# Which item of an expert is the full one, and the mask over its rows: a fused encoder layer with a mixture of experts

## Chip, cores and metric

One NeuronCore of a Trainium2 chip runs the whole layer in one launch. The metric is the device time in microseconds (us); lower is better. No other core takes part.

## The reference, cut to what matters

One layer: attention and a pooling mixer on 1024 tokens of width 1024, then a router that gives each token 4 of 32 experts, and a clamped SwiGLU expert on the rows it was given. Only the last part is touched:

```
logits = hf @ w_router + b_router;  topv, topi = top_k(logits, 4);  gates = softmax(topv)
for each expert e, for the rows of the tokens that chose e:
    g = min(xb @ w_gate[e] + b_gate[e], 7);  u = clip(xb @ w_up[e] + b_up[e], -7, 7)
    y = ((u + 1) * (g * sigmoid(1.702 * g))) @ w_down[e] + b_down[e]
    out[token] += y * gate
```

The three matrices of an expert are 1024x1024 in float32, so 12.6 MB per expert. The router's choice for these inputs, counted by evaluating the reference, gives the experts 0 to 31 this many rows: 135, 167, 108, 69, 133, 141, 71, 217, 126, 117, 91, 185, 46, 158, 74, 161, 157, 75, 210, 102, 117, 94, 60, 103, 182, 109, 128, 190, 148, 157, 111, 154. The order in which an expert's rows are computed does not change the result beyond rounding.

## The kernel before, in words

The kernel first does attention, output projection, router and the tables of the expert part (the first 620 us). Then all five engines run one hardware loop each over **items**. An item is up to 128 rows (CHUNK) of one expert; an expert with n rows has ceil(n / 128) items, 47 in all here. 15 experts have two items, 17 have one. The items stand in order of the expert, and the table of items gives for each the expert, the rank of its first row (`first`) and a number from which its **kind** follows. Before, the expression `shift = cnt - 128 * endi` makes this number the rank of the item's last row: the first item of an expert holds the remainder (1 to 128 rows), every later item is full.

TensorE (`item`, L1369 on) has four bodies of code, for items of at most 32, 64, 96 and 128 rows; it reads the number from the table and branches. The smaller kinds use column tiles of the array, so they need fewer cycles. I write "a 32", "a 64", "a 96" and "a 128" for items of these kinds. The kinds in the order before, one expert between bars (from the counts above, the remainder standing first):

32 128 | 64 128 | 128 | 96 | 32 128 | 32 128 | 96 | 96 128 | 128 | 128 | 96 | 64 128 | 64 | 32 128 | 96 | 64 128 | 32 128 | 96 | 96 128 | 128 | 128 | 96 | 64 | 128 | 64 128 | 128 | 128 | 64 128 | 32 128 | 32 128 | 128 | 32 128

An item on TensorE: bias (L1396, its first matmul), gate and up projections over the input rows k 0 to 3, then 4 to 7 (L1402), transposes of the hidden rows (L1412), down projection (L1427 for a 128, L1444 for a 64, L1465 for a 32, both of the last for a 96), among them the transposes of the next item's gathered rows (L1338, two halves) and the matmuls that find the rows of the item after it (L1330).

The weights have a single buffer, and SyncE reloads it in four parts as the **last item of an expert** lets go of them: both upper halves of gate and up (4 MB) after that item's k 0 to 3 (L439), both lower halves after its gate and up, half of w_down after half of its down projection, the rest after its end (L446):

```
done = sp.value_load(ends[0:1, bass.ds(e - 1, 1)], ...)
sp.wait_ge(s_k03, done)
```

VectorE (`with dve.Fori(0, MAX_ITEMS)`) at the start of item j makes the pick matrix for item j + 2: `item_slots` (L989 to L992) masks the ranks that lie beyond that item's last row and subtracts `first`, then `compare` (L996) compares with 0 to 127. After this `places` (L1012 on) waits for TensorE. Behind the SwiGLU work it waits until the rows of item j - 1 have been added in memory (`dve.wait_ge(s_added, j + 1)`), and then copies the places and gates of item j (L1121, L1122, L1065), which release ScalarE's scaling of the output rows (L765), moves the next item's rows (L1061), turns the found rows into numbers (L1006 to L1003) and chooses the next expert's bias row (L1023). The next item's first matmul waits for that last step. VectorE and ScalarE do four SwiGLU units for every kind, the unused ones too.

GpSimd gathers the rows of item j + 2 (L600) and adds the output rows of item j to memory with four indirect DMAs (L632), waits for all four and signals `s_added`.

Of the kernel before, what the change touches and what calls it, by code (L numbers as in the profile page):

```python
# [27 lines left out]
ALU = mybir.AluOpType  # L28
# [4 lines left out]
SEQ = 1024  # L33
# [13 lines left out]
CHUNK = 128  # L47
# [4 lines left out]
TABLE = MAX_ITEMS + 2  # L52
# [10 lines left out]
def encoder_kernel(nc, t, out):  # L63

    with ExitStack() as ctx:
# [3 lines left out]
        def sem(name):  # L69
            return ctx.enter_context(nc.semaphore(name))  # L70
# [107 lines left out]
        slot = Z[:, 18432:18688].rearrange("p (i e) -> p i e", i=TT)  # L178
# [7 lines left out]
        def small(cols):  # L186
            taken[0] += cols
            assert taken[0] <= 12288
            return Z[:, taken[0] - cols:taken[0]]
# [8 lines left out]
        b_r, cnt, nit, endi, shift, onese, is_exp, ejunk, iota_e = (small(EXPERTS) for _ in range(9))  # L198
        gsum, ginv, iota_p, iota_t, missing, limits = (small(c) for c in (8, 8, 1, 1, 1, 7))
        of_p, ofc, less = (small(c) for c in (4, 1, 1))  # L200
# [6 lines left out]
        col = small(8)  # L207
# [10 lines left out]
        items = small(3 * TABLE)[0:1, :].bitcast(I32)  # L218
        ends = small(EXPERTS)[0:1, :].bitcast(I32)
        bounds = Z[:, 17536:17536 + 3 * TABLE]  # L220
        last_of, first = bounds[:, 0:TABLE], bounds[:, 2 * TABLE:]
        total = small(1)[0:1, :].bitcast(I32)


# [93 lines left out]
        s_c2 = sem("router_constants_ready")  # L318
# [173 lines left out]
        def _(pl):  # L492
# [53 lines left out]
            for step_no in range(UNITS + 2):  # L546
                u = step_no - 2

                h, i = divmod(step_no, TT)
# [28 lines left out]
            exact = dict(allow_small_or_imprecise_dtypes=True)  # L578
            pl.iota(iota_e, [[1, EXPERTS]], base=0, channel_multiplier=0, **exact).then_inc(s_c2, 1)
            pl.iota(iota_p, [[1, 1]], base=0, channel_multiplier=1, **exact).then_inc(s_c2, 1)  # L580
            pl.iota(iota_t, [[1, 1]], base=CHUNK, channel_multiplier=CHUNK, **exact).then_inc(s_c2, 1)
            pl.iota(iota_c, [[1, CHUNK]], base=0, channel_multiplier=0, **exact).then_inc(s_c2, 1)
            pl.iota(limits, [[CHUNK, 7]], base=CHUNK, channel_multiplier=0, **exact).then_inc(s_c2, 1)
            pl.iota(missing, [[1, 1]], base=SEQ + 1, channel_multiplier=1, **exact).then_inc(s_c2, 1)
# [195 lines left out]
        def _(dve):  # L780
            step = [0]

            def link(ins):
                step[0] += 1
                ins.then_inc(s_dve, 1)
                dve.wait_ge(s_dve, step[0])
# [200 lines left out]


            def item_slots(chain, e, n):  # L989
                own = slot[:, :, e].rearrange("p i e -> p (i e)")  # L990
                chain(dve.scalar_tensor_tensor(col, own, last_of[:, n], own, ALU.is_le, ALU.mult))
                chain(dve.tensor_scalar(col, col, first[:, n], None, ALU.subtract))  # L992

            def compare(dst=pickT):
                for i in range(TT):
# [26 lines left out]
            def choose(e):  # L1022
                dve.tensor_scalar(chosen[0:3 * EXPERTS, :], onesb[0:3 * EXPERTS, :],  # L1023
                                  of_row[0:3 * EXPERTS, e], None, ALU.mult).then_inc(s_chosen, 1)
# [15 lines left out]
            dve.tensor_copy(ends, endi[0:1, :]).then_inc(s_tab, 1)  # L1040
            link(dve.tensor_copy(total, endi[0:1, EXPERTS - 1:EXPERTS]))

            link(dve.scalar_tensor_tensor(shift, endi, -float(CHUNK), cnt, ALU.mult, ALU.add))
            link(dve.tensor_scalar(is_exp, endi, iota_p, None, ALU.is_le))
            link(dve.tensor_reduce(of_p[:, 0:1], is_exp, AX_X, ALU.add))
            link(dve.tensor_scalar(of_p[:, 0:1], of_p[:, 0:1], float(EXPERTS - 1), None, ALU.min))
            link(dve.tensor_scalar(is_exp, iota_e, of_p[:, 0:1], None, ALU.is_equal))
            link(dve.tensor_tensor_reduce(out=ejunk, in0=is_exp, in1=shift, scale=1.0, scalar=0.0, op0=ALU.mult,
                                          op1=ALU.add, accum_out=ofc))
            link(dve.tensor_tensor(of_p[:, 1:2], ofc, iota_t, ALU.add))  # L1050
            link(dve.tensor_scalar(less, of_p[:, 1:2], 33.0, None, ALU.is_lt))
            link(dve.scalar_tensor_tensor(of_p[:, 2:3], of_p[:, 1:2], 97.0, less, ALU.is_lt, ALU.add))
            link(dve.tensor_scalar(of_p[:, 3:4], of_p[:, 1:2], 1.0 - CHUNK, 1.0, ALU.add, ALU.max))
            for n in range(4):
                dve.tensor_scalar(diag[:, n * TABLE:(n + 1) * TABLE], ident[:, 0:TABLE], of_p[:, n:n + 1], None,
                                  ALU.mult).then_inc(s_diag, 1)
# [15 lines left out]
            e1 = dve.value_load(items[0:1, 1:2], min_val=0, max_val=EXPERTS - 1)  # L1072
            kind0 = dve.value_load(items[0:1, 2 * TABLE:2 * TABLE + 1], min_val=0, max_val=KINDS - 1)
            item_slots(link, slice(0, 1), slice(0, 1))
            compare(pick0)
            dve.wait_ge(s_pick, 2)
            item_slots(link, bass.ds(e1, 1), slice(1, 2))
            compare()
            choose(slice(0, 1))
# [8 lines left out]
            dve.sem_inc(s_ucl, UNIT)  # L1088

            LOOP0 = step[0]  # L1090
            PER = 11
            n_items = dve.value_load(total, min_val=EXPERTS, max_val=MAX_ITEMS)
            with dve.Fori(0, MAX_ITEMS) as j:
                with dve.If(j < n_items):
                    local = [0]

                    def chain(ins):
                        local[0] += 1
                        ins.then_inc(s_dve, 1)
                        dve.wait_ge(s_dve, j * PER + (LOOP0 + local[0]))  # L1100

                    e1 = dve.value_load(items[0:1, bass.ds(j + 1, 1)], min_val=0, max_val=EXPERTS - 1)
                    e2 = dve.value_load(items[0:1, bass.ds(j + 2, 1)], min_val=0, max_val=EXPERTS - 1)
                    kind = dve.value_load(items[0:1, bass.ds(j + (2 * TABLE + 1), 1)], min_val=0, max_val=KINDS - 1)
                    item_slots(chain, bass.ds(e2, 1), bass.ds(j + 2, 1))
                    compare()
                    places(chain, j + 1, kind)
# [21 lines left out]
                    choose(bass.ds(e1, 1))  # L1129
                    assert local[0] == PER  # L1130

# [469 lines left out]
```

## Time and profile before

| what | us |
|---|---|
| median of 3 runs | 2505.13 (2503.92 to 2511.53) |
| the profiled execution, its own time | 2503.77 |
| its span | 2502.0 |
| loop over the items, first matmul of the first item to ScalarE's first output scaling of the last | 1845.15 (619.90 to 2465.05) |

The profile tells when each engine was busy with what and what released it after a wait. A row of the order of time reads: start, duration, engine, line, operation, and in brackets how long the engine had been idle and what ended it; "issue" means that nothing the profile shows was waited for.

### The profile page before, as it was taken

The numbers are of one execution on the slowest core, as the hardware profiler recorded it, in microseconds if no ns is written. First come the engines' busy times: TensorE is split into PE (matmuls) and PEld (weight loads), VectorE is DVE, ScalarE is ACT, GpSimd is POOL, SyncE is SP. The second block draws the span as 40 slices with busy tenths as digits, with TensorE's granted clock in tenths as the row PEclk, the third lists the DMA queues.
The fourth block names the chain that finished last, engine by engine and source line by source line (L and its number), as shares of the span: only waits on it lengthen the run. The fifth ranks groups of instructions, "written<-read, shape, count | busy, mean of one in ns | idle before, by whom it ended". The sixth has DMA issues, their size and how long they took to land.

```text
span 2502.0 us, 30088 instructions
## 1 busy us (share of the span) xinstructions
PE 2254.2 (90%) x9757; PEld 1054.0 (42%) x9758; DVE 859.1 (34%) x2563; ACT 475.5 (19%) x1006; POOL 508.0 (20%) x442
## 2 busy tenths in 40 slices
PE   8999899995789889999989899899998999989984
PEld 4444677553334344334433334334443344334431
DVE  2012888345323233232233323323222323233233
ACT  1000787210111111111111111111111101111112
POOL 1031463102121112211121221221112111222121
PEclk9999999996889999999989999999998999999997
DMA  7000011414347856938859694593889668567754
GB/s 267 9 1 29 39 68 51 158 65 188 113 141 288 329 184 198 344 98 330 310 167 342 205 342 155 194 339 104 332 305 366 223 230 302 163 222 235 270 182 151
DMA packets 149247, 502.78 MB, mean 201 GB/s; under 512 B 10170, under 2 KB 34767, under 8 KB 147631
## 3 DMA queue, kind: packets, MB, share of 16 engines
q1 hardware_dynamic: 113200, 446.79, 46.8%
q0 software_dynamic: 34128, 50.35, 10.2%
q10 hardware_dynamic: 1874, 5.02, 0.5%
q8 instruction: 31, 0.51, 0.1%
q14 instruction: 14, 0.11, 0.0%
HBM read 463.82 MB, written 42.50 MB: 202 GB/s over the span
## 4 chain that ended last, share of the span: by engine, by line
PE 82%; DVE 7%; issue 6%; DMA 2%; POOL 2%; ACT 2%; DVEq 0%; ACTq 0%; POOLq 0%
PE psum L1402 40%; PE psum L1427 13%; PE psum L1179 9%; PE psum L1237 4%; PE psum L1444 3%; PE psum L1465 2%; PE psum L1338 2%; PE psum L1396 2%; PE psum L1412 2%; DMA weights<-in_w_down 1%; DVE work L880 1%; POOL osq L563 1%; PE psum L1330 1%; PE psum L1226 1%; PE psum L1295 1%
## 5 line engine op out<-in xcount | busy, mean ns | idle before, releaser
L1402 PE MATMUL psum<-weights,work 128*128 128x512 f32 (+2 forms) x3520 | 1065.2, 617 | 0.0
L1402 PEld LDWEIGHTS psum<-weights,work 128*128 128x128 f32 (+2 forms) x3520 | 399.1, 158 | 530.3 <-issue 523.3
L1427 PE MATMUL psum<-weights,work 128*128 128x512 f32 x768 | 347.4, 595 | 0.0
L600 POOL DMA_INDIRECT work<-normed_rows,work x49 | 49.6, 1011 | 1408.8 <-DVE work L1003 1097.7
L632 POOL DMA_INDIRECT residual_rows<-work x188 | 294.8, 1568 | 123.2 <-ACT work L765 72.6
L758 ACT ACTIVATE work<-work 128x256 f32<-128x256 f32 x188 | 77.3, 411 | 809.2 <-DVE work L1111 809.2
L1179 PE MATMUL psum<-weights 128*128 128x512 f32 x512 | 220.5, 593 | 2.6 <-DVE weights L823 2.6
L1427 PEld LDWEIGHTS psum<-weights,work 128*128 128x128 f32 x768 | 140.0, 190 | 141.4 <-issue 137.9
L1012 DVE TENSOR_REDUCE work<-psum 128x8 f32 x48 | 8.8, 184 | 485.9 <-PE psum L1352 485.9
L1111 DVE TENSOR_SCALAR work<-psum 128x256 f32<-128x256 f32 x188 | 79.5, 423 | 272.0 <-PE psum L1402 272.0
L760 ACT ACTIVATE work<-psum 128x256 f32<-128x256 f32 x188 | 71.6, 381 | 443.3 <-PE psum L1412 443.3
L1396 PE MATMUL psum<-work 96*128 96x512 bf16 (+2 forms) x220 | 58.6, 414 | 104.0 <-issue 104.0
L1179 PEld LDWEIGHTS psum<-weights 128*128 128x128 f32 x512 | 97.0, 190 | 125.0 <-issue 121.9
L765 ACT ACTIVATE work<-psum,work 128x256 f32<-128x256 f32 x188 | 73.8, 475 | 342.6 <-PE psum L1427 255.5
L1061 DVE TENSOR_TENSOR work<-psum,gains 128x512 f32<-128x512 f32 x96 | 66.4, 691 | 168.0 <-PE psum L1338 161.5
L1444 PE MATMUL psum<-weights,work 128*64 128x512 f32 x480 | 109.0, 595 | 3.3 <-ACT work L760 3.3
L1237 PE MATMUL psum<-weights 128*128 128x512 f32 x256 | 111.8, 594 | 0.0
L1115 DVE TENSOR_TENSOR work<-work 128x256 f32<-128x256 f32 x188 | 80.0, 426 | 83.8 <-ACT work L758 81.4
L996 DVE TENSOR_SCALAR work<-work 128x128 bf16<-128x128 f32 x400 | 86.4, 299 | 1.8
L1117 DVE SCALAR_TENSOR_TENSOR work<-work 128x256 f32<-128x256 f32 x188 | 79.9, 425 | 6.5
L880 DVE CUSTOM_DVE_ANT_0 work<-psum,weights 128x1024 f32<-128x1024 f32 x64 | 78.1, 1221 | 6.0 <-PE psum L1226 5.4
L833 DVE TENSOR_SCALAR work<-psum 128x512 f32<-128x512 f32 x16 | 11.1, 691 | 199.3 <-PE psum L1179 199.3
(199 smaller groups left out, 1795.8 us busy)
## 6 DMA issues: line engine op xcount, KB each, us to landing
weights<-in_w_gate SPq DMA_DIRECT2D x64, 2048.0 KB, 7.8
weights<-in_w_up SPq DMA_DIRECT2D x64, 2048.0 KB, 12.4
weights<-in_w_down SPq DMA_DIRECT2D x64, 2048.0 KB
x<-in_x SPq DMA_DIRECT2D x16, 512.0 KB, 6.6
weights<-in_w_in SPq DMA_DIRECT2D x8, 1024.0 KB, 15.6
residual_rows<-x SPq DMA_DIRECT2D x9, 512.0 KB, 2.6
normed_rows<-work ACTq DMA_DIRECT2D x9, 512.0 KB, 2.7
bias_rows_repeated<-bias_rows SPq DMA_DIRECT2D x4, 1024.0 KB, 9.7
```

Source lines behind the costliest of these rows:

```text
L632: pl.indirect_dma_start(acc_d[:, :], bass.IndirectOffsetOnAxis(dest[:, b:b + 1], 0), yrow[:, b * BLK:(b + 1) * BLK], None, compute_op=ALU. ...
L880: dve.tensor_tensor_reduce(out=prob[:, u % SETS, m, :], in0=PS[:, 2 * m * HALF:(2 * m + 2) * HALF], in1=bias[:, h, at:at + SEQ], scale=1.0 ...
L996: last = dve.tensor_scalar(dst[:, i, :], iota_c, col[:, i:i + 1], None, ALU.is_equal)
L1111: dve.tensor_scalar(gmin[:, b, :], bank(b, BLK), LIMIT, None, ALU.min).then_inc(s_gm, 1)
L1115: dve.tensor_tensor(sig[:, b, :], gmin[:, b, :], sig[:, b, :], ALU.mult).then_inc(s_sg, 1)
L1117: dve.scalar_tensor_tensor(hid[:, b, :], ucl[:, b, :], 1.0, sig[:, b, :], ALU.add, ALU.mult).then_inc(s_hid, 1)
L1179: return pe.matmul(bank(4 + n % 4), lhs, rhs, start=(k == 0), stop=(k == DT - 1))
L1237: mm = pe.matmul(bank(n % 4), mixT[:, c, i * P:(i + 1) * P], w_out[:, c, q * HALF:(q + 1) * HALF], start=(c == 0), stop=(c == DT - 1))
L1396: pe.matmul(out, chosen[0:3 * EXPERTS, 0:cols], bgu[:, :, blk * BLK:(blk + 1) * BLK], start=True, stop=False)
L1402: mm = pe.matmul(out.rearrange("p (m n) -> p m n", m=2), xT[:, k, lo:lo + cols], wgu[:, :, k, blk * BLK:(blk + 1) * BLK], start=False, sto ...
L1427: mm = pe.matmul(bank(4 + h), actT[:, k, :], wdn[:, k, h * HALF:(h + 1) * HALF], start=False, stop=(k == DT - 1))
L1444: mm = pe.matmul(PS[64 * h:64 * h + 64, 4 * HALF:5 * HALF], actT[:, 2 * b + s, 64 * c:64 * c + 64], wdn[:, k, h * HALF:(h + 1) * HALF], st ...
```

## The change

The table of items now starts from the first row of the expert's first item: `shift` is 128 times the number of items before the expert, `first` is 1 + 128 * (p - items before), and the number from which the kind follows is the count of the expert's rows that are left when item p begins, clamped to 0..1024. So an expert's first item is full when it has more than one, and its last holds the remainder. Ranks beyond an item's 128 rows now give a column of 128 or more, which no comparison meets, so the masking instruction of `item_slots` goes. The order of kinds is now:

128 32 | 128 64 | 128 | 96 | 128 32 | 128 32 | 96 | 128 96 | 128 | 128 | 96 | 128 64 | 64 | 128 32 | 96 | 128 64 | 128 32 | 96 | 128 96 | 128 | 128 | 96 | 64 | 128 | 128 64 | 128 | 128 | 128 64 | 128 32 | 128 32 | 128 | 128 32

```diff
-        last_of, first = bounds[:, 0:TABLE], bounds[:, 2 * TABLE:]
+        first = bounds[:, 2 * TABLE:]
...
-            pl.iota(iota_t, [[1, 1]], base=CHUNK, channel_multiplier=CHUNK, **exact).then_inc(s_c2, 1)
+            pl.iota(iota_t, [[1, 1]], base=0, channel_multiplier=CHUNK, **exact).then_inc(s_c2, 1)
...
             def item_slots(chain, e, n):
-                own = slot[:, :, e].rearrange("p i e -> p (i e)")
-                chain(dve.scalar_tensor_tensor(col, own, last_of[:, n], own, ALU.is_le, ALU.mult))
-                chain(dve.tensor_scalar(col, col, first[:, n], None, ALU.subtract))
+                chain(dve.tensor_scalar(col, slot[:, :, e].rearrange("p i e -> p (i e)"), first[:, n], None,
+                                        ALU.subtract))
...
-            link(dve.scalar_tensor_tensor(shift, endi, -float(CHUNK), cnt, ALU.mult, ALU.add))
+            link(dve.tensor_tensor(shift, endi, nit, ALU.subtract))
+            link(dve.tensor_scalar(shift, shift, float(CHUNK), None, ALU.mult))
+            link(dve.tensor_tensor(cnt, cnt, shift, ALU.add))
...
-            link(dve.tensor_tensor(of_p[:, 1:2], ofc, iota_t, ALU.add))
+            link(dve.tensor_tensor_reduce(out=ejunk, in0=is_exp, in1=cnt, scale=1.0, scalar=0.0, op0=ALU.mult,
+                                          op1=ALU.add, accum_out=of_p[:, 1:2]))
+            link(dve.tensor_tensor(of_p[:, 1:2], of_p[:, 1:2], iota_t, ALU.subtract))
+            link(dve.tensor_scalar(of_p[:, 1:2], of_p[:, 1:2], 0.0, float(SEQ), ALU.max, ALU.min))
...
-            link(dve.tensor_scalar(of_p[:, 3:4], of_p[:, 1:2], 1.0 - CHUNK, 1.0, ALU.add, ALU.max))
+            link(dve.tensor_scalar(ofc, ofc, -1.0, 1.0, ALU.mult, ALU.add))
+            link(dve.tensor_tensor(of_p[:, 3:4], ofc, iota_t, ALU.add))
...
-            PER = 11
+            PER = 10
```

On VectorE, the start of the item loop before: the loads of the table, the mask (L991), the subtraction (L992), the eight comparisons and the wait for TensorE's matmuls.

```order
507 L1104 TENSOR_LOAD work
508 L1104 ISA x2
509 L991 ISA
510 L991 SCALAR_TENSOR_TENSOR work<-work 128x8
511 L1100 ISA
512 L992 ISA
513 L992 TENSOR_SCALAR work<-work 128x8
514 L1100 REGISTER_ALU
515 L996 TENSOR_SCALAR work<-work 128x128 x8
```

The same place in the changed kernel, whose lines are numbered one less here.

```order
510 L1109 TENSOR_LOAD work
511 L1109 ISA x2
513 L990 ISA
514 L990 TENSOR_SCALAR work<-work 128x8
515 L1105 ISA
516 L995 TENSOR_SCALAR work<-work 128x128 x8
```

One instruction of 128x8 is gone from each item; nothing else on VectorE has moved in the loop. On VectorE, the making of the item table ahead of the loop, before:

```order
453 L1041 CAST work<-work 1x1
454 L1043 SCALAR_TENSOR_TENSOR work<-work 128x32
455 L1044 TENSOR_SCALAR work<-work 128x32
459 L1048 ISA work<-work 128x32
460 L1048 ISA work 128x1
461 L1050 TENSOR_TENSOR work<-work 128x1
462 L1051 TENSOR_SCALAR work<-work 128x1
463 L1052 SCALAR_TENSOR_TENSOR work<-work 128x1
464 L1053 TENSOR_SCALAR work<-work 128x1
465 L1055 TENSOR_SCALAR work<-ident,work 128x66 x4
```

The same place in the changed kernel:

```order
454 L1042 TENSOR_TENSOR work<-work 128x32
455 L1043 TENSOR_SCALAR work<-work 128x32
456 L1044 TENSOR_TENSOR work<-work 128x32
463 L1051 ISA work<-work 128x32
464 L1051 ISA work 128x1
465 L1053 TENSOR_TENSOR work<-work 128x1
466 L1054 TENSOR_SCALAR work<-work 128x1
469 L1057 TENSOR_SCALAR work<-work 128x1
470 L1058 TENSOR_TENSOR work<-work 128x1
471 L1060 TENSOR_SCALAR work<-ident,work 128x66 x4
```

The first expression has become three instructions, a second masked sum (L1051, an instruction and the reading of its accumulator) and a clamp (L1054) have come in, and one instruction has become two (L1057, L1058). The other engines have the same instructions; which of TensorE's bodies of code an item takes is decided by the table at run time.

## Rows read from the trace of the kernel before

**Rows 1.** The page: shares of the chain of work that ended last, by engine.

```profile
PE 82%; DVE 7%; issue 6%; DMA 2%; POOL 2%; ACT 2%; DVEq 0%; ACTq 0%; POOLq 0%
```

**Rows 2.** Item starts on TensorE in order of time: 96, 96, 128, 128.

```profile
1635.43 0.41 PE L1396 MATMUL psum<-work 96*64 96x512 bf16 x2
1674.75 0.61 PE L1396 MATMUL psum<-work 96*64 96x512 bf16 x2 [3.73 <-issue]
1715.36 0.39 PE L1396 MATMUL psum<-work 96*128 96x512 bf16 x1 [3.33 <-issue]
1761.91 0.38 PE L1396 MATMUL psum<-work 96*128 96x512 bf16 x1
```

**Rows 3.** Item starts on TensorE in order of time: 128, 64, 128, 32, 128, 32.

```profile
2092.76 0.38 PE L1396 MATMUL psum<-work 96*128 96x512 bf16 x1
2137.70 0.41 PE L1396 MATMUL psum<-work 96*64 96x512 bf16 x2
2167.60 0.61 PE L1396 MATMUL psum<-work 96*128 96x512 bf16 x1 [3.65 <-issue]
2215.29 0.40 PE L1396 MATMUL psum<-work 96*32 96x512 bf16 x4
2236.82 0.61 PE L1396 MATMUL psum<-work 96*128 96x512 bf16 x1 [3.68 <-issue]
2284.04 0.40 PE L1396 MATMUL psum<-work 96*32 96x512 bf16 x4
```

**Rows 4.** Item starts on TensorE: a 64 behind a 96, then a 128.

```profile
1266.07 0.64 PE L1396 MATMUL psum<-work 96*64 96x512 bf16 x2 [3.56 <-issue]
1298.91 0.60 PE L1396 MATMUL psum<-work 96*128 96x512 bf16 x1 [3.64 <-issue]
```

**Rows 5.** Down projection's first matmul in small items: all grouped (count, busy, mean ns, idle before), and one.

```profile
L1459 PE MATMUL psum<-work 96*32 96x256 bf16 x64 | 4.9, 295 | 13.5 <-DMA weights<-in_w_down 8.4 <-ACT work L760 5.1
...
1393.60 0.41 PE L1459 MATMUL psum<-work 96*32 96x256 bf16 x4 [5.15 <-DMA weights<-in_w_down]
```

**Rows 6.** Item starts on TensorE: the 128 behind that waiting 32, and the next item.

```profile
1403.33 0.39 PE L1396 MATMUL psum<-work 96*128 96x512 bf16 x1 [2.90 <-issue]
1448.28 0.41 PE L1396 MATMUL psum<-work 96*64 96x512 bf16 x2
```

**Rows 7.** VectorE in the loop: mask, and the wait behind it; count, busy, mean ns, idle before.

```profile
L991 DVE SCALAR_TENSOR_TENSOR work<-work 128x8 f32 x47 | 10.9, 232 | 125.2 <-issue 125.2
L1012 DVE TENSOR_REDUCE work<-psum 128x8 f32 x47 | 8.7, 184 | 485.2 <-PE psum L1352 485.2
```

**Rows 8.** ScalarE in order of time: output scaling of the 32 that starts at 2215.29.

```profile
2230.99 1.20 ACT L765 ACTIVATE work<-psum,work 128x256 f32<-128x256 f32 x3 [1.25 <-DVE work L1065]
```

**Rows 9.** Last adding DMA in that 32, no weights in flight: issue, and time to landing.

```profile
2223.39 1.56 POOL L632 DMA_INDIRECT residual_rows<-work  x1 [0.30 <-issue]
residual_rows<-work POOLq DMA_INDIRECT x1, 4.0
```

**Rows 10.** SyncE's issue at 1353; adding DMA's landing at 1353.8 and 1381; page's weight landing.

```profile
1353.55 0.38 SPq L439 DMA_DIRECT2D weights<-in_w_gate  x1
residual_rows<-work POOLq DMA_INDIRECT x1, 7.8
residual_rows<-work POOLq DMA_INDIRECT x1, 8.9
weights<-in_w_up SPq DMA_DIRECT2D x64, 2048.0 KB, 12.4
```

**Rows 11.** Starts of the second, fourth, sixth item; the page's queue of TensorE's instruction loads.

```profile
650.64 0.60 PE L1396 MATMUL psum<-work 96*128 96x512 bf16 x1 [11.04 <-issue]
734.11 0.61 PE L1396 MATMUL psum<-work 96*128 96x512 bf16 x1 [10.53 <-issue]
831.28 0.41 PE L1396 MATMUL psum<-work 96*64 96x512 bf16 x2 [4.62 <-issue]
q8 instruction: 31, 0.51, 0.1%
```

## The prediction

> **What bounds the kernel now.** I read the page first: TensorE has 82% of the chain that ended last [rows 1], and VectorE, ScalarE, GpSimd and the DMA queue each have slack on average. So the question is how long TensorE takes from the first matmul of one item to that of the next, and how this interval depends on what stands before it. The second view is therefore the order of time on TensorE at the starts of items (L1396). I write a|b for the interval of an a that stands behind a b. A 128|128 takes 2137.70 - 2092.76 = 44.9 us, a 64|128 29.9, a 128|64 47.7, a 32|128 21.5 (2236.82 - 2215.29), a 128|32 47.2 [rows 3]. A 96|96 takes 40.6 and a 96|128 39.3, a 128|96 46.5 [rows 2], a 64|96 32.8 [rows 4]. The reader is to see two things. Each kind has its own length, so moving an item inside its expert changes nothing at first. But an item behind a smaller one starts after a pause of 3.3 to 3.7 us that nothing in the profile ended: it comes behind the choice of the next expert's bias, which a 128 prepares ahead of its last matmuls and the smaller kinds only after them. And it runs longer: a 128 by 1.6 us (behind a 96) or by 2.3 to 2.8 (behind a 32 or 64), a 96 by 1.3, a 64 by 2.9.
>
> The third view groups what ended the waits inside items. For weights, the first matmul of a small item's down projection waits 8.4 us in all, 5.15 of it in one 32; the usual releaser is ScalarE, 5.1 us over all others [rows 5].
>
> **The change part by part.** The sum is made against the profiled execution (2503.77 us; the median shown is 1.4 higher); minus is faster.
>
> *The mask.* One instruction of 232 ns per item, with its hand-over some 0.4 us; 47 of them are 18 us of VectorE's time. But behind the comparisons VectorE waits for TensorE's L1352, 485 us over 47 items, 10 each [rows 7]. That wait grows by 0.4 each: **0**. Without this cover it would be -18.
>
> *Weights that came late.* A remainder that stands first meets weights whose last part is still under way; standing last it uses what its expert has long had. Two 32s hold the 8.4 us, of which about 1.5 would be spent anyway, so -6.9. But the 128 behind the first of them took only 1448.28 - 1403.33 = 44.9 us after a pause of 2.9 [rows 6], without the 2.3 that a 128|32 pays; I take the same for the other, and give back 2.3 each and some tenths of pause. Net **-1.5** (ends -6.9 and 0).
>
> *Who stands behind whom.* From the two lists of kinds: before, 14 128s stand behind a 32 or 64 and 2 behind a 96; 3 64s, 2 96s and 2 32s stand behind a smaller item, the first item aside. After, it is 10 and 7 128s, 2 64s, 3 96s and no 32. With 2.3, 1.6, 2.9, 1.3 and for a 32 1.8 (about the mean of these, an estimate), the extras are 32.2 + 3.2 + 8.7 + 2.6 + 3.6 = 50.3 before and 23.0 + 11.2 + 5.8 + 3.9 = 43.9 after: **-6** (ends -8 and -4, as a 96 behind a 32 or a 64 behind a 64, which no row shows, may cost 1 more each, and the 128's extra is between 2.3 and 2.8).
>
> *The end of the loop.* The last item is now a 32, and the last needs no pause behind it. ScalarE's output scaling begins 2230.99 - 2215.29 = 15.7 us after the start of a 32 [rows 8], 5.8 before the next start would be; behind a last 128 there is no such rest. **-6**. What comes after the loop is the same.
>
> *The adding of the rows.* This is the price of the new order. While a 32 runs behind a 128, GpSimd adds the rows of that 128, and VectorE may pass its wait for this at L1121, the first of three copies of 0.2 us ahead of the scaling at +15.7: at +15.0. Before, the 32 is an expert's first, so the next weights aren't asked for: the last of the four DMAs is issued at +8.1 and lands 4.0 later, at +12.1, and VectorE isn't held up [rows 9]. After, the 32 is its expert's last, and SyncE asks for the next expert's gate and up, 8 MB, from about +4 on. In a 64 where this was so already (weights asked for at 1353.55) the last adding DMA took 7.8 us, in another stretch with weights 8.9 [rows 10]. That makes +15.9 to +17.0, and some tenths until VectorE knows of it: it is 1 to 2.5 late. Late next are the scaling, the move of the next rows and so the next item's start, one behind the other. Seven 32s have this (the eighth is the last item, with no weights behind it): 7 to 17. I take 1.6 each, near the 64's row, since that is the same place in the program: **+11**. A 64 or 96 reaches L1121 later and keeps its cover. The low end is 0, if the four DMAs get through as they did without weights.
>
> *Do the next weights come in time behind a remainder?* A 32 lets the first quarter go 4 us after its start and ends its interval at 21.5; the 4 MB land in 12.4 [rows 10], at +16.4: 5 us of cover. All 12.6 MB took 40 us from issue to use in the tightest stretch (1353.55 to 1393.60) [rows 5, 10], so they are there at +44. The down projection begins when about two thirds of a 128 are over and 0.6 of a smaller kind (gate and up against the whole of its matmuls): for a 128 at 21.5 + 31 = +52, for a 96 at +46. The tightest is expert 12's 64 behind expert 11's 64: asked for at +7.5, there at +47.5, wanted at 29.9 + 19 = +49. **0**; without the cover it is 2 us at that one place.
>
> *Loading TensorE's code.* The starts of the second, fourth and sixth item have idle times of 11.04, 10.53 and 4.62 us, where a 128 behind a 32 or 64 has 3.7 later on and one behind a 128 none; TensorE's code came in 31 loads, 0.51 MB together [rows 11]. Over those the three hold 7.3 + 6.8 + 4.6 = 19 us. Each was among the first entries into its body by a jump. They stay, in another order. New is that the first item of all is a 128, whose code lies behind all other bodies, while a 32's follows on the loop's head. The nearest row is the sixth item's: **+4** (ends -7, if one of the two dear entries into the 128 goes with this, and +11, if it costs what they did). The Trainium skill ("Runtime: NRT & Kernel Launch", Instruction fetch mechanics) says that a taken branch to a page outside a window of two pages waits for the page's load. By that rule every change of kind would stall all through the loop, which is rival 2's direction; the trace shows such stalls in the first six items and none in the later rows.
>
> *The table.* Six instructions more for it and two masks fewer, 0.23 us each as the mask: 1.4 - 0.5 = **+1**. TensorE waits for this chain ahead of the first item.
>
> Sum: 0 - 1.5 - 6 - 6 + 11 + 0 + 4 + 1 = **+2.5**. That is 2506.3 for the profiled execution and on the median 2508 us.
>
> **The rivals.**
> 1. *The adding of rows stays covered.* For it: without weights in flight it has 3 us to spare. Against: both stretches with weights. The sum is then 2.5 - 11 = -8.5, 2497 on the median; with no new stall for code -12.5, 2493. This is the other side of no change. It decides from where the last DMA takes under 6.5 us. 0.14.
> 2. *Code loads cost much more.* If the first 128 pays 11 and the first 32 and the first 96 behind it pay 4.6 each, it is 16 over my sum: 2524; with one of these alone 2513 to 2515. For it: no jump from a 128 back into a 32 comes among the first six items before. Against: the third item entered the 64 from a 128 without a stall among those rows. 0.15.
> 3. *The remainder is too short a cover for the weights.* A 32 gives 18 us to a load of 40, where the full item gave 42. If adding, gathering and weights slow each other so that the first 4 MB take more than 17.5 us, each us beyond it costs 7, once for each 32: at 20 us it is +17, 2525. Against: 12.4 is the median over loads with adding in flight too. 0.08.
> 4. *The mask was on the path:* -18, 2490. Only if VectorE's start of an item set TensorE's pace, which its 10 us of wait exclude. 0.02.
>
> The forecast has 0.61.
>
> **How the numbers follow.** 0.3%, 7.5 us, is about what a measurement of this kernel can tell from no change. The forecast's own range is 2500 to 2515. The whole range reaches to 2496 for rival 1 and to 2520 for rivals 2 and 3. Faster than 2497.6: most of rival 1 and rival 4, 0.15. Slower than 2512.6: rivals 2 and 3 and a little of the forecast (the adding at its high end), 0.25. Within: 0.60.
>
> **What would show it right or wrong.** In the changed kernel L1121 should stand behind a wait for the adding DMA in seven 32s, 1 to 2.5 us each, and their intervals be 22.5 to 24 instead of 21.5; no wait for w_down should be left; a 128|96 should be 46.5, seven times; the last scaling should come 15.7 us after its item's start. The first item's start shows the code's part. Wrong would be: waits for w_gate or w_up at L1402, pauses of "issue" above 4 us beyond the sixth item, or no wait at L1121.

## The result and the profile after

The changed kernel takes 2525.58 us (2524.68 to 2531.07, 4 runs) against 2504.97 before: ratio 1.0081, 95% interval 1.0059 to 1.0104. It is slower by 20.6 us, where I had forecast 2.5 to 3 more and a range up to 2520. The profiled execution took 2524.68, its span is 2522.9: 20.9 more than before. I explain these 20.9.

In all rows below lines of VectorE up to L1042 are one lower than before, from L1066 on five higher: L1121 is now L1126, L1396 is L1401, L1402 is L1407. The page of the changed kernel, with the rows that answer to [rows 1, 7, 11] and the landing of weights:

```profile
span 2522.9 us, 29951 instructions
PE 2253.9 (89%) x9757; PEld 1055.9 (42%) x9758; DVE 854.3 (34%) x2520; ACT 475.0 (19%) x1006; POOL 506.3 (20%) x442
q8 instruction: 32, 0.52, 0.1%
PE 79%; DVE 7%; issue 7%; DMA 3%; POOL 3%; ACT 2%; DVEq 0%; ACTq 0%; POOLq 0%
L1011 DVE TENSOR_REDUCE work<-psum 128x8 f32 x48 | 8.8, 184 | 509.5 <-PE psum L1357 509.5
weights<-in_w_up SPq DMA_DIRECT2D x64, 2048.0 KB, 14.3
```

TensorE does the same work (9757 matmuls) and has less of the chain, 79% instead of 82%; GpSimd and DMA each have one point more. The first place to look is the wait that the prediction named. The grouped view of VectorE's L1126 says how often the engine stood still ahead of it and for whom:

```profile
L1126 DVE CAST work<-work x47: 160/163/171, 659.3 to 2483.2; 128x4 uint32<-128x4 f32 x47
its engine sat idle before it (us, times) until:
  POOLq L637: 17.8, 7
```

Before, nobody held it up there:

```profile
L1121 DVE CAST work<-work x47: 161/161/165, 636.7 to 2451.0; 128x4 uint32<-128x4 f32 x47
its engine sat idle before it (us, times) until:
who waited for it (us, times):
```

L637 is GpSimd's signal that an item's rows are added. One of the seven items in the order of time: its start on TensorE, the last adding DMA's issue, its landing time, the late L1126, the next start.

```profile
2280.87 0.40 PE L1401 MATMUL psum<-work 96*32 96x512 bf16 x4
2288.92 1.55 POOL L632 DMA_INDIRECT residual_rows<-work  x1 [0.30 <-issue]
residual_rows<-work POOLq DMA_INDIRECT x1, 8.8
2297.91 0.17 DVE L1126 CAST work<-work 128x4 uint32<-128x4 f32 x1 [1.94 <-POOLq L637]
2304.40 0.61 PE L1401 MATMUL psum<-work 96*128 96x512 bf16 x1 [3.63 <-issue]
```

The DMA is issued at +8.1 as before [rows 9], but lands 8.8 later instead of 4.0 (in the seven it is 8.8 to 9.8); L1126 runs at +17.0 instead of +15.0, and the next item starts at +23.5 instead of +21.5. The six 32s with such a follower, the second item aside, took 24.6, 24.5, 24.7, 24.6, 23.5 and 23.5.

The other place is the first five items. TensorE's starts there, with the pause that nothing ended, as in [rows 11]:

```profile
626.27 0.61 PE L1401 MATMUL psum<-work 96*128 96x512 bf16 x1 [8.43 <-issue]
703.92 0.61 PE L1401 MATMUL psum<-work 96*128 96x512 bf16 x1 [9.56 <-issue]
792.88 0.61 PE L1401 MATMUL psum<-work 96*128 96x512 bf16 x1 [15.34 <-issue]
844.38 0.41 PE L1401 MATMUL psum<-work 96*64 96x512 bf16 x2 [4.16 <-issue]
```

These are the first, third, fifth and sixth item. Over what such starts cost otherwise (3.9 at the first, 3.7 behind a small item, 0 behind a 128) the pauses hold 4.5 + 5.9 + 11.6 + 4.2 = 26.2 us; before it was 18.7. The loads of code stop where these pauses stop. Of the 32 loads 17 come ahead of the loop; the window from 618 to 900 us has the other 15, the last at 885.0, and no later window has one (before, 14 in the loop, the last at 871.9):

```profile
q8 instruction: 15, 0.25, 0.3%
```

### The profile page after: what moved, and what is told of

It reads as the page before. It is cut to its first block, busy times and chain, and to the rows that moved or that the text cites. A ratio compares the mean times of both kernels' runs of the same rounds, so it can differ in the third digit from the quotient of the medians.

```text
span 2522.9 us, 29951 instructions
## 1 busy us (share of the span) xinstructions
PE 2253.9 (89%) x9757; PEld 1055.9 (42%) x9758; DVE 854.3 (34%) x2520; ACT 475.0 (19%) x1006; POOL 506.3 (20%) x442
## 4 chain that ended last, share of the span: by engine, by line
PE 79%; DVE 7%; issue 7%; DMA 3%; POOL 3%; ACT 2%; DVEq 0%; ACTq 0%; POOLq 0%
PE psum L1407 39%; PE psum L1432 13%; PE psum L1184 9%; PE psum L1242 4%; PE psum L1449 3%; DMA residual_rows<-work 3%; PE psum L1343 2%; PE psum L1401 2%; DVE work L880 1%; PE psum L1417 1%; POOL residual_rows L632 1%; PE psum L1470 1%; POOL osq L563 1%; PE psum L1231 1%; PE psum L1335 1%
## 5 line engine op out<-in xcount | busy, mean ns | idle before, releaser
L1407 PE MATMUL psum<-weights,work 128*128 128x512 f32 (+2 forms) x3520 | 1066.6, 612 | 0.0
L1407 PEld LDWEIGHTS psum<-weights,work 128*128 128x128 f32 (+2 forms) x3520 | 400.9, 158 | 529.1 <-issue 521.9
L1011 DVE TENSOR_REDUCE work<-psum 128x8 f32 x48 | 8.8, 184 | 509.5 <-PE psum L1357 509.5
L1401 PE MATMUL psum<-work 96*128 96x512 bf16 (+2 forms) x220 | 58.6, 408 | 109.8 <-issue 109.8
L1066 DVE TENSOR_TENSOR work<-psum,gains 128x512 f32<-128x512 f32 x96 | 66.4, 691 | 162.6 <-PE psum L1343 156.1
L1343 PE MATMUL psum<-ident,work 128*128 128x128 f32 x384 | 62.7, 288 | 39.2 <-DVE work L1066 39.2
## 6 DMA issues: line engine op xcount, KB each, us to landing
weights<-in_w_down SPq DMA_DIRECT2D x64, 2048.0 KB, 11.6
```

Of the source, the lines that this page charges most:

```text
L1343: mm = pe.transpose(bank(7, P, c * P), xg[:, k * P:(k + 1) * P], ident[:, :])
L1401: pe.matmul(out, chosen[0:3 * EXPERTS, 0:cols], bgu[:, :, blk * BLK:(blk + 1) * BLK], start=True, stop=False)
L1407: mm = pe.matmul(out.rearrange("p (m n) -> p m n", m=2), xT[:, k, lo:lo + cols], wgu[:, :, k, blk * BLK:(blk + 1) * BLK], start=False, sto ...
```

## The experiments

The theories: **A**, the adding DMAs are slowed by the next expert's weights, and the small item's follower waits for them; **code**, the loading of TensorE's code by far jumps; against them **B**, it is the place in the expert and not the weights, and the mask or weight waits.

**1. The mask put back.**

```diff
-                chain(dve.tensor_scalar(col, slot[:, :, e].rearrange("p i e -> p (i e)"), first[:, n], None,
-                                        ALU.subtract))
+                own = slot[:, :, e].rearrange("p i e -> p (i e)")
+                chain(dve.scalar_tensor_tensor(col, own, 0.0, own, ALU.is_ge, ALU.mult))
+                chain(dve.tensor_scalar(col, col, first[:, n], None, ALU.subtract))
...
-            PER = 10
+            PER = 11
```

> The changed kernel with one instruction of 128x8 put back where the mask stood (it multiplies the ranks by 'not negative', so it changes no value). If the mask's time is hidden behind VectorE's wait for TensorE (10 us per item), the time stays at 2525 (within 3). If VectorE's start of an item is on the path, it is 47 x 0.4 = 18 us more, 2543.

2528.23 us (2525.9 to 2529.95), ratio to before 1.0093, 1.0076 to 1.0110. Its interval overlaps that of the changed kernel (1.0059 to 1.0104): no 18 us. In the traces the loop is as long with the mask as without it, 1841.6 us from the first item's start to the last's against 1841.9; the 2.2 us between the profiled executions lie ahead of the first item. The grouped wait shows where the time went; it stands at 494.9 where the changed kernel has 509.5, over 48 instructions:

```profile
L1012 DVE TENSOR_REDUCE work<-psum 128x8 f32 x48 | 8.8, 184 | 494.9 <-PE psum L1358 494.9
```

That is 0.3 us per item: the mask takes its own time out of a wait, as said.

**2 and 3. Nearly no weights in flight, in both orders.**

```diff
-                    load_gu(m, 0, bass.ds(e, 1))
+                    tiny_gu(m, 0, bass.ds(e, 1))
...
+            def tiny_gu(m, half, e):
+                src = wgu_d[m][:, e, 4 * half, 0:8].rearrange("p e n -> p (e n)")
+                sp.dma_start(wgu[:, m, 4 * half, 0:8], src).then_inc(s_wk[half], 16)
```

(and the same for the other three loads). Both kernels leave out the weights of all experts but the first; they are there for their times alone.

> The changed kernel, but from the second expert on each weight load brings 8 columns of one row block only (left out: the weights of all experts but the first; the work on every engine stays). Theory A, the adding DMAs are late because the next expert's weights are in flight: the wait ahead of L1126 (17.8 us over 7 items) is gone and a 32 behind a 128 takes 21.5 us again instead of 23.5 to 24.8; about 19 us less than the changed kernel's 2525, so 2506. Rival B, it is the position in the expert or the order of GpSimd's work, not the weights: intervals of 24 us remain, 2524.

> The kernel before, with the same cut of the weight loads. Its late w_down (8.4 us of wait in two items) goes, but the items behind start colder: 2503 by both theories. Theory A then has the two orders 3 us apart once no weights are in flight (code loads +9, end of the loop and colder starts -8 to -10, table +1), rival B 20.

One execution each: 2500.06 (span 2498.2) and 2496.32 (span 2494.6). The orders are 3.6 us apart instead of 20.9. Without weights the new order gains 24.7 and the old one 7.4. In the new order the wait ahead of the three copies is gone, and a 32 behind a 128 takes 21.5 to 21.9 again. The same item as above, with L1409 as its first matmul and L1134 as VectorE's first copy:

```profile
2262.00 0.40 PE L1409 MATMUL psum<-work 96*32 96x512 bf16 x4
2277.01 0.16 DVE L1134 CAST work<-work 128x4 uint32<-128x4 f32 x1
2283.48 0.60 PE L1409 MATMUL psum<-work 96*128 96x512 bf16 x1 [3.62 <-issue]
```

Theory A holds and B falls. The new order came out 6 us below what I had expected of it, and the old one 7 us below its 2503, and in good part for the same reason. A second thing came out there, which I had not looked for: the pauses of the first items became shorter too. The third and fifth item:

```profile
701.91 0.61 PE L1409 MATMUL psum<-work 96*128 96x512 bf16 x1 [8.14 <-issue]
787.14 0.61 PE L1409 MATMUL psum<-work 96*128 96x512 bf16 x1 [11.09 <-issue]
```

With weights in flight it was 9.56 and 15.34, and the sixth item's pause fell from 4.16 to 2.53. The 15.34 is no accident of one execution: experiments 1, 4 and 8, which have weights and the same code, show 15.51, 15.36 and 15.38. In the old order the long pauses of the second and fourth item come when hardly any weights are asked for, and they barely changed (11.04 and 10.53 became 10.41 and 10.20); the sixth's, with weights under way, went from 4.62 to 2.08. In the fourth item three pages of code are loaded with weights and without; each is under way for about 1 us either way. But they start 29.6, 35.5 and 38.9 us after the item's start instead of 27.6, 31.9 and 34.6, which makes the 4.3 us. What holds up their start is not shown.

Ahead of the first item these executions are less alike: with the same code and nearly the same pause it starts at 629.1 here, at 626.3 in the changed kernel.

**4. VectorE's wait moved off TensorE's path, new order.**

```diff
-                    dve.wait_ge(s_added, j + 1)
-                    chain(dve.tensor_copy(dest, nextitem[:, 0:4]))
-                    chain(dve.tensor_copy(dgate, nextitem[:, 4:8]))
-                    shift_places(j + 1)
                     move_xT(j + 1)
...
                     choose(bass.ds(e1, 1))
+                    dve.wait_ge(s_added, j + 1)
+                    chain(dve.tensor_copy(dest, nextitem[:, 0:4]))
+                    chain(dve.tensor_copy(dgate, nextitem[:, 4:8]))
+                    shift_places(j + 1)
+                    dve.tensor_copy(less, new)
```

The last line is a copy of one column that nothing reads later; it takes 0.15 us.

> The changed kernel with VectorE's wait for the added rows and the three copies behind it moved behind the move of the next rows, the row numbers and the choice of the expert. TensorE's next item then no longer hangs on that wait. Theory A: the 17.8 us of wait leave the path, and each small item (22 that have a follower) is 0.6 us shorter as the three copies leave it too: 2525 - 19 - 13 = 2493. Rival C, the stall is only passed on (GpSimd adds the small item's rows later, and the next item hangs on its gather): little gain, 2515 or more.

2497.77 us (2494.27 to 2500.05), ratio 0.9967, 0.9953 to 0.9981: 28 less than the changed kernel, and faster than the kernel before. The gain is near what was worked out, 32, so the stall is not just passed on (rival C). A 32 behind a 128 takes 20.8 to 21.9. Where it fell short shows in the grouped waits, a row that the changed kernel does not have (L1403 is the first matmul here):

```profile
PE psum L1403 <- DMA weights<-in_w_up: 20.9, 5, 4.7
```

and in one of those starts:

```profile
2283.57 0.39 PE L1403 MATMUL psum<-work 96*128 96x512 bf16 x1 [3.71 <-DMA weights<-in_w_up]
```

The next expert's first weights now land last, after a pause of 3.7 that would be there anyway. So rival 3 (a remainder is too short a cover) is a real second limit that lay just behind the first; the five pauses are 3.7 to 4.7, so it costs up to 1 us per item here.

**5. The same move in the old order.** The diff is that of experiment 4.

> The kernel before (remainder first, mask in), with the same move of VectorE's wait and copies as in the changed kernel's version that reached 2498. In the old order that wait never held, so by theory A only the three copies leave the path: 23 x 0.6 = 13 us, 2492, and the old order stays 5 us ahead of the new one. Rival D, the move helps for another reason than the wait: then it gives the old order as much as the new one, 27 us, 2478.

2494.72 us (2492.17 to 2497.29), ratio 0.9954, 0.9937 to 0.9971: 10 to 11 less than before. The move gives the new order 28 and the old one 11. The part that both have I put down to the three copies (13 expected; most of the small items are 0.7 us shorter); the other 17 fit the wait that only the new order has, 17.8 us. Rival D, the same gain in both orders, falls.

**6 and 7. The full item's code first.**

```diff
-                    with pe.If(n_tok < 97):
-                        with pe.If(n_tok < 33):
...
+                    with pe.If(n_tok > 96):
+                        item(j, e, e2, 128)
+                    with pe.Else():
+                        with pe.If(n_tok < 33):
```

> The changed kernel with TensorE's body for full items placed first in the loop's code instead of last; no other edit. If the loading of code by a far jump is what the first items pay for (start of the first item 5 us late, 6, 12 and 5 us in the second, fourth and fifth), the first item starts at 621 instead of 626.3 and the loop loses 5 to 20 us: 2510 to 2520. If those delays have another cause, nothing moves: 2525.

> The kernel before with the same placing of the full items' body. Here the first item is a 32, whose code then lies behind the full body. By the code theory its start (619.9) gets 4 to 6 us later, and the dear entries into the full body (7 us each, two) go: 2495 to 2508. If the cause is another: 2505.

New order: 2506.50 us (2503.13 to 2507.7), ratio 1.0002, 0.9988 to 1.0015: 19 less than the changed kernel and below the 2510 to 2520 I had expected. Old order: 2491.80 (2489.78 to 2494.91), ratio 0.9943, 0.9925 to 0.9961: 13 to 14 less than before. It is the largest single gain in the old order, and lies below the 2495 to 2508 I had expected. The loads of code, new order first (32 before), then old order (31 before):

```profile
q8 instruction: 27, 0.44, 0.1%
```

```profile
q8 instruction: 25, 0.41, 0.1%
```

And the first start in the new order, where the full item's code now follows on the loop's head; the pause is 3.83 instead of 8.43:

```profile
622.32 0.61 PE L1401 MATMUL psum<-work 96*128 96x512 bf16 x1 [3.83 <-issue]
```

In the old order the first start moved the other way, from 619.91 with 3.93 to this, as the code theory has it for a 32 whose code has moved to the far side:

```profile
625.14 0.62 PE L1396 MATMUL psum<-work 96*32 96x512 bf16 x4 [8.18 <-issue]
```

The loop won it back at the second and fourth item (7.25 and 7.22 instead of 11.04 and 10.53), and the sixth item's 4.62 is gone. But the code of the first items is not the whole gain. At the start of the eighth item the old order is 9.2 us ahead, of 13.4 in the span, and the new one 16.6 of 20.6; in the new order the second item's wait for the adding, 3.1, is gone too. The rest comes later, where no code is loaded: in the new order the pause ahead of a 128 behind a 96 is 2.9 us instead of 3.3, and three of the seven then take 44.9 instead of 46.6. The first 5.4 us of one of them, in the changed kernel and here; behind the times of the five engines stand TensorE's granted clock, the share of the DMA engines and GB/s:

```profile
1155.20:1160.60 5.40, 5.40 (x10) 2.26 (x11) 2.19 (x9) 0.00 (x0) 4.49 (x4) 0.68 1.00 388
1137.40:1142.80 5.40, 5.40 (x14) 2.54 (x15) 2.20 (x9) 0.00 (x0) 4.66 (x3) 1.00 1.01 391
```

The clock stayed at 1.00 (2.4 GHz), and TensorE got through 14 matmuls instead of 10. So the place of the code also sets how long the pause in front of an item is, and a shorter pause can leave the clock up; behind the other four of the seven, with the same pause, it was 0.68 to 0.74.

**8. The next weights held back until the rows are added, new order.**

```diff
                 sp.wait_ge(s_k03, done)
+                sp.wait_ge(s_added, done)
```

> The changed kernel, but SyncE asks for the next expert's first weights only when the rows of the item before the expert's last are added (for a 32 some 8 us later than now; for larger last items hardly ever later). Theory A: no wait is left ahead of L1126, since the adding DMAs run alone; but the first 4 MB then land at +25 of a 32 behind a 128, later than the next start at +21.5, so 3 to 4 us move to a wait for weights at the next item: intervals of 25, time 2522 to 2530. Rival B (not the weights): the wait ahead of L1126 stays at 17 us in all and the weight waits come on top, 2545.

2534.18 us, one execution. The wait ahead of the copies is gone, as A says and against B; the same time and more stands at the next expert's start:

```profile
PE psum L1402 <- DMA weights<-in_w_up: 60.2, 7, 10.3
```

The upper end of what I expected was 2530. Six of the pauses are 8.0 to 8.7 us, 3.7 of which are there in any case (the 10.3 is the third item's, which loads code too), and the 32s take 25.8 to 26.6. So one after the other, the adding of 0.5 MB of rows and the first 4 MB of weights do not fit in a small item's 21 us; beside each other, as in experiment 4, they overrun it by 1 us at most.

**9 and 10. Both edits, in both orders.** The diffs are those of experiments 4 and 6.

> The old order with both edits, VectorE's wait and copies moved and the full items' body first. If wait and code loads are separate causes the gains add: 2505 - 11 - 14 = 2480.

> The new order with both edits. Separate causes: 2525.5 - 28 - 19 = 2479, level with the old order under the same edits or a few us ahead (no late w_down, the last item a 32). If code and wait were the whole of the change's price, the two orders differ by less than 5 us. If the new order has a further cost, such as waits for w_gate and w_up at the next expert's start, it stays 5 to 10 us behind.

Old order: 2473.32 us (2470.25 to 2477.35), ratio 0.9871, 0.9856 to 0.9886, 7 us better than the sum of the two gains; where these 7 come from is not shown. New order: 2479.26 (2477.69 to 2486.39), ratio 0.9907, 0.9893 to 0.9921, as the sum said. The two intervals stay just apart, and by medians the old order is 6 us faster, which was the case of a further cost. The two profiled executions cannot show it: they are the old order's slowest and the new one's fastest, with spans of 2475.6 and 2475.9. The new order is the one with waits for weights at L1403, 24.8 us in 6 items; 3.6 or so of each would be a pause anyway, so some 3 us of the 6 could be theirs, and the rest stays open:

```profile
PE psum L1403 <- DMA weights<-in_w_up: 24.8, 6, 4.6
```

The best kernel of the case is number 9, the old order with both edits, 32 us or 1.3% faster than before. It needs neither the new order nor the dropped mask.

## Why the prediction was wrong

Its terms again, with what the two traces give for each (us, plus is slower):

| term | forecast | measured |
|---|---|---|
| the mask | 0 | 0 |
| weights that came late | -1.5 | -1.5 |
| who stands behind whom | -6 | -2.5 |
| the end of the loop | -6 | -4 |
| the adding of the rows | +11 | +19.5 |
| cover for the next weights | 0 | 0 |
| code | +4 | +7.5 |
| the table | +1 | +1.8 |
| sum | +2.5 | +20.8 of 20.9 |

**The step that failed most is "I take 1.6 each, near the 64's row".** The mechanism, its place, the number of items and the later price were right: seven waits, L1121, one after the other to the next start. The size was not. The waits are 1.9 to 3.1, 2.5 each (17.8 in 7), and six intervals grew by 145.4 - 6 x 21.5 = 16.4, so 2.7 each; with the second item's 3.1 it is 19.5. That lies not only over my +11 but over the upper end of the term, 17. I had two rows for the landing, 7.8 and 8.9, and took the lower because it is "the same place in the program", a 64 whose weights are asked for 0.3 us ahead of the last adding DMA. The changed kernel has that place five times, and there the last DMA lands 8.9 to 9.9 after its issue. One of them, its start, the request for weights, the adding DMA and its landing:

```profile
2203.96 0.41 PE L1401 MATMUL psum<-work 96*64 96x512 bf16 x2
2211.75 0.38 SPq L439 DMA_DIRECT2D weights<-in_w_gate  x1
2212.01 1.55 POOL L632 DMA_INDIRECT residual_rows<-work  x1 [0.30 <-issue]
residual_rows<-work POOLq DMA_INDIRECT x1, 9.9
```

So the 7.8 was no price of the place but one low row, and in the 32s it is 8.8 to 9.8. The 7.8 came where the last part of the weights before had been asked for only 7.7 us ahead of the new ones; whether that made it lower, no run shows. Nor was the 4.0 of [rows 9] quite without weights: between 2223.3 and 2224 their queue still moved 0.07 MB. Experiment 2 has 3.7 to 3.9 with nearly none. Experiments 2, 4 and 8 each take away one side of the meeting, weights or wait, and the stall goes.

**Code: right in sign, half in size.** I added the cheapest row, 4.6 at one start. The first start paid just that (4.5), but the entries behind it paid too: 5.9, 11.6 and 4.2, where before it was 7.3, 6.8 and 4.6. The 15.34 at the fifth item is the surprise. Experiment 2 shows that 4.3 of it come from weights in flight, since 11.09 remain without. I had counted the code's loads as a price of the jump alone and not as transfers that cost more beside weights. Experiments 6 and 7 move nothing but the place of the code and gain 19 and 14, so the place of the code is a cause; the difference of these gains, 5 to 6, is near the +7.5, but 3.1 of the 19 are the second item's wait, and a part of both gains lies behind the first items. Which page is loaded when, and why a second entry into the full body pays again, stays open. The page of the Trainium skill that I cited ("Runtime: NRT & Kernel Launch", Instruction fetch mechanics) says that a taken branch out of a window of two pages waits for its page. By that every change of kind would stall; the trace does not agree: no page is loaded after 885.0, while the kinds change through 40 more items.

**Who stands behind whom.** My 1.3 for a 96 behind a small item came from behind a 96; behind a 32 it is 1.8 to 2.5 (41.2, 40.7 and 41.4 against 38.9), and the pause ahead of it is 4.0. A 128 behind a 32 takes 47.4 to 47.8, so 2.6 and not 2.3. The seven 128s behind a 96 took 46.5 to 46.7 as forecast. The starts of such a 96 and of the item behind it:

```profile
1028.41 0.64 PE L1401 MATMUL psum<-work 96*64 96x512 bf16 x2 [4.02 <-issue]
1069.63 0.39 PE L1401 MATMUL psum<-work 96*128 96x512 bf16 x1 [3.31 <-issue]
```

Before, the extras are 49.3 (forecast 50.3), after 46.8 (forecast 43.9). What an extra is, the windows show: the first 5.4 us of a 128 behind another 128, then of the 128 that starts at 2304.40 behind a pause of 3.63. The columns are those of the windows in experiments 6 and 7:

```profile
2159.00:2164.40 5.40, 5.40 (x15) 2.56 (x14) 1.89 (x9) 2.85 (x5) 2.53 (x2) 1.00 1.02 408
2304.40:2309.80 5.40, 5.40 (x7) 2.33 (x8) 2.21 (x9) 0.00 (x0) 4.49 (x4) 0.51 1.03 409
```

Behind the pause TensorE has a granted clock of 0.51, near its lower level (1.2 GHz), and gets through 7 matmuls, where it does 15 at 1.00 (2.4 GHz). That costs about half of these 5.4 us.

**The end of the loop.** The last scaling does start 15.7 after the item's start, at 2483.89. But what follows is not the same, as I had said. In order of time on GpSimd:

```profile
2487.87 1.01 POOL L600 DMA_INDIRECT work<-normed_rows,work  x1 [10.07 <-DVE work L1002]
2489.18 1.58 POOL L632 DMA_INDIRECT residual_rows<-work  x1 [0.30 <-issue]
```

GpSimd's loop gathers for item j + 2 before it adds the rows of item j, and in a 32 the row numbers for that gather come after the scaling. So the adding starts 5.3 us behind the scaling, where behind a last 128 it was 2.4. Until the end of the span it is 39.0 instead of 36.9.

**The table.** The +1.8 is 626.27 - 619.91 less the 4.5 of code. It is read from one execution each, and the start of the first item moves by up to 3 us between executions of the same code up to there (625.7 to 629.1), so one execution hardly measures a term of this size.

**Right:** the mask (experiment 1); no wait for weights in any item of the changed kernel; no late w_down. But the cover was nearly gone: the first 4 MB landed 20.0 to 21.0 us after such a 32's start and not at +16.4, because the load took 15.4 to 16.3 from the issue of its second half and not 12.4. Against the +21.5 at which the next start used to come that is 0.5 to 1.5 us of cover instead of 5. Rival 3 was wrong for this kernel by that little: with the adding and the copies off the path it shows (experiments 4 and 10). Rival 1 is dead, and rival 2 is right in part. Rivals 2 and 3 had 2524 and 2525, which is what was measured, but not what happened: the time came from the adding and, less, from code and from who stands behind whom. The chances had 0.25 for slower, and the reasons for it stood in the text; the low choice within the bounds of the largest term, and bounds from two rows, kept the range too short.

## What to carry to other kernels

A transfer that a wait hangs on has two prices, alone and beside the traffic that the change moves next to it. Where only two rows show the second, they are no bounds: here both the lower and the higher lay below most of what came. Let the sum be tried with more than the higher one. A pause of a few us on TensorE has a second price too, the lower clock behind it. Where a small piece of work must cover loads, a scatter and bookkeeping, ask for each in which order they land; taking the latest away shows the next. And first ask whether the wait has to be on the path at all: moving it behind the work that the other engine needs gave 28 us in the new order and 11 in the old.

## What the hardware showed that I had not expected

The last of an item's adding DMAs (four of 128 rows of 1 KB) landed 3.7 to 4.0 us after its issue with few or no weights in flight (experiment 2, [rows 9]), and 7.8 to 9.9 when the next 8 MB of weights were asked for ahead of it (the kernel before and the changed one). Pauses in which TensorE's code is loaded were longer beside weights (15.34 us with, 11.09 without). Where a body of code stands in a hardware loop with branches was worth 14 to 19 us of 2500, two thirds or more of it by the eighth item's start: the loads of 16 KB fell from 31 to 25 and from 32 to 27 with the full item's body first. A pause of 2.9 us left the granted clock at 1.00 three times out of seven; one of 3.3 left it at 0.68 over the next 5.4 us, one of 3.6 at 0.51.
